# Two transformer blocks on one core: seven levels of a gated linear attention placed in pairs among the banks of the projections

## The reference

```python
b = jnp.cumsum(gi.astype(jnp.float32), axis=2)
diff = b[:, :, :, None, :] - b[:, :, None, :, :]
decay = jnp.exp(jnp.where(causal[None, None, :, :, None], diff, -jnp.inf))
A = jnp.einsum('bhid,bhjd,bhijd->bhij', qf, kf, decay)
o_intra = jnp.einsum('bhij,bhje->bhie', A, vf)
...
o_g = rms_norm(o_g, g_norm[l]).reshape(B, T, G_WIDTH) * jax.nn.silu(rg)
```

## Time and profile before

| what | value |
|---|---|
| median of three runs | 1561.66 us (1561.66 to 1562.43) |
| the profiled execution | 1561.91 us |
| its span, first to last instruction | 1560.1 us |
| PE busy | 1544.7 us |
| DVE busy | 991.2 us |
| ACT busy | 667.5 us |
| POOL busy | 504.8 us |
| granted clock of TensorE | 0.999 |

### The profile page before, as it was taken

The page is one execution under the profiler, slowest core; times in us unless marked ns, Lnnn a source line. Parts: engine busy times, 40 slices in busy tenths (PEclk is TensorE's granted clock), DMA queues, the critical chain, the costliest instruction groups (busy, mean ns, idle before and its releaser), DMA issues.

```text
span 1560.1 us, 20969 instructions
## 1 busy us (share of the span) xinstructions
PE 1544.7 (99%) x7728; PEld 1298.3 (83%) x7728; DVE 991.2 (64%) x1192; ACT 667.5 (43%) x1096; POOL 504.8 (32%) x285
## 2 busy tenths in 40 slices
PE   8999999999999999999999999999999999999998
PEld 6888888888788888888888898988888988888886
DVE  5464875435477777876664747357356677777776
ACT  5352565244444443443533334543334454434442
POOL 2451000000037776765410000020013037777761
PEclk9999999999999999999999999999999999999999
DMA  6422135221312223222332232343334222213232
GB/s 246 151 71 80 41 109 186 85 82 54 135 54 108 108 108 108 108 108 69 128 101 85 59 95 68 95 149 112 108 115 156 93 103 81 94 61 119 83 110 79
DMA packets 44709, 160.16 MB, mean 103 GB/s; under 512 B 5552, under 2 KB 5752, under 8 KB 44240
## 3 DMA queue, kind: packets, MB, share of 16 engines
q1 hardware_dynamic: 40608, 144.82, 28.3%
q0 software_dynamic: 4016, 14.18, 2.6%
HBM read 156.80 MB, written 3.76 MB: 103 GB/s over the span
## 4 chain that ended last, share of the span: by engine, by line
PE 93%; DVE 3%; ACT 2%; DMA 1%; issue 1%; POOL 0%; DVEq 0%; ACTq 0%; SPq 0%; POOLq 0%
PE banks L1237 29%; PE banks L1239 29%; PE banks L1238 29%; PE banks L1532 1%; PE banks L1411 1%; DVE nmax L2210 1%; DVE w_lo L1941 1%; DMA w_raw<-in_weights 1%; PE banks L1349 0%; PE banks L1594 0%; DVE banks L2209 0%; PE banks L1570 0%; PE banks L1562 0%; PE banks L1521 0%; ACT w_hi L1630 0%
## 5 line engine op out<-in xcount | busy, mean ns | idle before, releaser
L1237 PE MATMUL banks<-act_hi,w_hi 128*128 128x512 f32 (+1 forms) x1088 | 413.4, 380 | 3.1 <-DVE act_lo L2092 3.1
L1239 PE MATMUL banks<-act_hi,w_lo 128*128 128x512 f32 (+1 forms) x1088 | 410.0, 377 | 0.0
L1238 PE MATMUL banks<-act_lo,w_hi 128*128 128x512 f32 (+1 forms) x1088 | 409.9, 377 | 0.0
L1941 DVE TENSOR_TENSOR w_lo<-w_raw,w_hi 128x1024 fp32r<-128x1024 f32 x208 | 271.2, 1310 | 187.4 <-ACT w_hi L1630 186.4
L1630 ACT ACTIVATE w_hi<-w_raw 128x1024 fp32r<-128x1024 f32 x208 | 218.5, 1059 | 241.8 <-DMA w_raw<-in_weights 189.3
L1237 PEld LDWEIGHTS banks<-act_hi,w_hi 128*128 128x128 f32 x1088 | 204.8, 188 | 41.2 <-DVE w_lo L1941 1.6
L1239 PEld LDWEIGHTS banks<-act_hi,w_lo 128*128 128x128 f32 x1088 | 204.7, 188 | 37.7
L1238 PEld LDWEIGHTS banks<-act_lo,w_hi 128*128 128x128 f32 x1088 | 204.8, 188 | 36.5
L1237 PE MATMUL banks<-w_hi,a_hi 128*128 128x512 f32 x392 | 152.7, 390 | 0.0
L1238 PE MATMUL banks<-w_lo,a_hi 128*128 128x512 f32 x392 | 152.6, 389 | 0.0
L1239 PE MATMUL banks<-w_hi,a_lo 128*128 128x512 f32 x392 | 152.5, 389 | 0.0
(11 more groups left out here) (345 smaller groups left out, 2410.2 us busy)
## 6 DMA issues: line engine op xcount, KB each, us to landing
w_raw<-in_weights SPq DMA_DIRECT2D x208, 512.0 KB, 3.6
w_down<-in_weights SPq DMA_DIRECT2D x56, 512.0 KB, 6.4
wide<-share_dram POOLq DMA_DIRECT2D x3, 1024.0 KB, 10.7
x_tok<-in_x SPq DMA_DIRECT2D x4, 512.0 KB, 5.1
w_first<-in_weights SPq DMA_DIRECT2D x4, 512.0 KB, 8.2
x_tok<-in_x POOLq DMA_DIRECT2D x4, 512.0 KB, 5.4
out<-x_tok SPq DMA_DIRECT2D x8, 256.0 KB, 2.0
skew_dram<-bias_dram POOLq DMA_DIRECT2D x1, 1536.0 KB, 12.1
```

The costliest lines, as they stand in the source:

```text
L1237: pe.matmul(out_ap, lhs[0], rhs[0], start=start, stop=False, skip_group_check=goes_on)
L1238: pe.matmul(out_ap, lhs[0], rhs[1], start=False, stop=False, skip_group_check=goes_on)
L1239: return pe.matmul(out_ap, lhs[1], rhs[0], start=False, stop=stop, skip_group_check=goes_on)
L1941: dve.tensor_tensor(w_lo[:, slot, :], landed(kind, raw), w_hi[:, slot, :], ALU.subtract).then_inc(lo_w, 1)
```

## The change

The loop over the seven levels hands out the same ten banks in another rhythm, as (banks ahead of level 0, 1, ... 6): before 0, 1, 2, 2, 2, 2, 1; after 1, 0, 4, 0, 4, 0, 1.

```diff
@@ -598,7 +598,7 @@
                   s.bank_steps("va", "tok", "act", banks_at=(0, 1, 2, 0)))
     go(steps, 2)
     for n in range(last):
-        go(steps, 0 if n == 0 else 1 if n in (1, last - 1) else 2)
+        go(steps, 0 if n % 2 else 1 if n in (0, last - 1) else 4)
         s.levels[n] = s.add("level", SIDE[n % 2 * 2:n % 2 * 2 + 2], n=n, ready=all_out())
         if n == 0:
             s.add("farprep")
```

## The result

The changed kernel takes 1564.63 us (median of 22 runs, 1562.82 to 1565.47), beside 1561.84 us for the kernel before on the same chips (22 runs, 1561.35 to 1563.25). The ratio is 1.0015, with a 95% interval of 1.0009 to 1.0021: slower by 1.4 to 3.3 us by that interval, and by 2.8 us by the medians. That is little, and at the edge of what such a measurement can tell from no change. The forecast was 1563.5, in a range of 1561.0 to 1565.0.

The account below looks back on a forecast made before the run. PE, busy for 99% of the span, was taken as the bound. Three pairs' gaps, -0.6 us, plus a new 2.5 us stall gave +1.9 us, so a median of 1563.5 us, range 1561.0 to 1565.0.

Parts of the forecast that it names:

- The removed gaps: On PE, pairing levels drops one exit and one entry gap, 0.2 us per pair; three pairs give -0.6 us.
- The moved work: Levels 0 to 6 regrouped: each engine's work moves along; level 0 one bank later on PE, by 5.44 us.
- the need at 96.09: On PE, qa0's 19th matmul needs the last weight unit, unit 3, at 96.09 us.
- DVE's rigid shift: In the first pair, farprep's products move 5.44 us later: k_far's from 87.07 to 92.51, q_far's from 88.21 to 93.65.
- ACT's 92.4 and POOL's 93.6: Level 3's exponential follows k_far's on ACT at 92.4 us; POOL's first multiplication of level 3 starts at 93.6.
- The turns: DVE and POOL alternate at SBUF: q_far's multiplication ends 1.2 us late, unit 3's w_lo is ready at 98.4.
- The wait: PE stalls in qa0 for unit 3's w_lo; the loss is 2.5 us, paid in full, once.
- The small stall: Rival: DVE's two multiplications precede POOL's turn, w_lo ready at 97.2; net +0.7 us, 1562.4; chance 0.21.
- The large stall: Rival: unit 3's w_lo loses one more turn to POOL; net +2.9 us, 1564.6; chance 0.13.
- The second stall at ka0: Rival: the chain from level 2 to unit 3's split exceeds 11.4 us; measurably slower from 12.6 us; chance 0.09.
- no stall at all: Rival: level 1's copies and unit 3's split come over 1.2 us earlier; only gaps go, 1561.1; chance 0.1.
- a wait past 120 us: Sign that the prediction is wrong: PE's waits after the change include one past 120 us.

Follow-up runs that it names:

- the two kernels that keep all pairs and have no wait: Changed kernel with farprep moved behind rg3: 1560.76 us, ratio 0.9993; changed kernel with only qa's unit 3 split moved ahead of level 0: 1560.59 us, ratio 0.9993.
- the first profile: The profiled execution of the changed kernel itself, nothing else altered: 1564.91 us, span 1563.1.
- the eleven later runs: The changed kernel measured once more, unaltered, on the chip of the other experiments: 1564.21 us, ratio 1.0015 to the kernel before.
- the two kernels concerned: The changed kernel, profiled at 1564.91 and 1563.36 us, and the kernel before with only levels 0 and 1 paired, profiled at 1564.13, 1565.78 and 1568.82 us.

## Why the prediction was right, and where its sum was off

**The removed gaps: right in kind, too small.** I put the three pairs at -0.6 us. They give 1.1, by the start of level 6 in the two kernels that keep all pairs and have no wait, and 0.75 for two pairs. A level takes 1.93 us up to the next kind of matmul, but 32 matmuls of it inside a pair take less: two levels take 3.71 and not 3.86. The two rows show that the 1.93 up to the next kind holds some 0.15 us that are not spent between two levels; I had taken them for part of the level, from a row in which the next group was of transposes. So a pair gives 0.35 and not 0.2.

**The moved work: right to 0.1 us.** PE's order, the need at 96.09 (the due time was 95.96), DVE's rigid shift (k_far's product at 92.51, q_far's at 93.65, measured 92.51 and 93.66), ACT's 92.4 and POOL's 93.6 all came as worked out. That level 1's operands are no limit held, and no later unit was late: neither ka0 nor va0 has an entry among the waits.

**The turns: right.** One turn was lost at q_far's product (2.29 us), none at w_lo, and the low part was ready at 98.30 for a forecast of 98.4. Both were close: POOL's product began at 93.60 and q_far's at 93.66, w_lo at 97.09 and POOL's subtraction at 97.15, so that by the same turns 0.06 us the other way would have given the small or the large stall; no run shows these two orders by themselves. The kernel in which POOL comes later shows the price by itself: with its 1.22 us for the product the wait is 0.9 shorter. The Trainium skill (SBUF — State Buffer, Who interferes with whom) states that a VectorE instruction with two SBUF inputs contends with a GpSimd instruction that reads SBUF, and that one with at most one SBUF input, outside the 2-port modes, does not. The traces agree with both: the products of q_far and of level 3 take 2.29 and 2.25 us beside each other, for 1.22 and 1.27 alone, and the masked copies, whose data come from PSUM, take 1.32 to 1.36 us beside POOL.

**The wait: right, and its price incomplete.** The loss of 2.5 us by the wait and its long first step was measured as 2.4 + 0.1. That it is paid in full holds as well, and that it is paid only once up to the 0.2 us at kx named below. The term that was missing is what the clock does in and behind the wait. My sum counted a late PE as late, but running at full speed from there on. In the first profile 1.5 us more were lost at 0.50 of the clock; in the profile of the same kernel at 1563.36 us none. The sum of the measured terms is -1.1 + 2.5 = +1.4 without and +2.9 with it. The runs lie in two such groups, 9 of 22 up to 1563.62 and 13 from 1564.17, whose medians (1563.31 and 1564.91) are 1.5 and 3.1 us over before, and the median of all falls into the upper one. The mean clock of each run goes with it: 0.999 or 1.000 in all nine and 0.998 in all 13, where some 3 us at the lower level are 0.001 of the span. In the eleven later runs one of the upper group, 1565.07, shows 1.000 all the same. My 1563.5 owes its closeness to two errors of opposite sign: 0.5 too little gain for the pairs, and 1.5 too little loss for the clock in the runs where it falls.

**The rivals.** The small stall (DVE ahead of POOL) did not come by itself, but was made, and gave +0.4 us by the medians and +0.5 by level 6, for the +0.7 worked out. The large stall's time, 1564.6, is the one measured, by another mechanism than the one named. The second stall at ka0 did not come. Its unit 3 was ready at 123.02 for a matmul at 125.73, 2.7 us in time where 1.2 to 1.9 were worked out:

```profile
121.30 1.72 DVE L1941 TENSOR_TENSOR w_lo<-w_raw,w_hi 128x1024 fp32r<-128x1024 f32 x1 [3.71 <-ACT w_hi L1630]
125.73 0.39 PE L1237 MATMUL banks<-act_hi,w_hi 128*128 128x512 f32 x1
```

That there is no stall at all was made in two ways, and gives 1560.6 to 1560.8. One sign of being wrong came in name only: a wait past 120 us, the 0.2 us for a copy of kx past 200 us. PE's weight load waits for that copy in every kernel, 0.2 us before and 0.3 to 0.6 where there is a wait at unit 3; what links the two was not followed up.

**What stays open.** Why the same wait of 2.2 us is followed by a half clock in one execution and not in the next is not settled, nor why it ends after 3 us in one and after 10 in another. Nor is it the change alone that brings a low clock: two of the 22 runs of the kernel before beside the later ones, 1563.21 and 1565.64, have a mean clock of 0.998 and 0.997. In the five profiles of the two kernels concerned the wait itself is 2.23 or 2.24 us, so the length of the wait does not tell them apart; what does was not found. In the three with a low stretch the clock fell some 0.15 us ahead of the late matmul twice, and 0.6 us behind it once.

## What to carry to other kernels

When steps are regrouped, look for the instruction whose place in a side engine's list moves behind a block of work, and set its end against the bank that needs it: here one split was 2.4 us late, while all the grouping was worth 1.1. The repair that keeps the gain is to move that one instruction ahead. Where PE is the bound, a new wait of two microseconds can cost more than its length, since the clock may halve inside or behind it; a sum for such a change should carry that term as a case of its own.

## What the runs showed of the hardware that was not expected

A wait of PE of 1.3 us (1.5 against the due time) was followed by full clock in its profile, and its 11 runs lie within 1.5 us, all with a mean clock of 0.999 or more. A wait of 2.2 was followed by full clock in two profiles and by the lower level in three, lasting some 3 us in two of them and 10 us in one. In those of 3.65 and 4.43 the clock fell to the lower level before PE was back, at 99.8 and 99.0 for matmuls at 100.06 and 100.84, and all six runs of each lie above 1565.8, with a mean clock of 0.997 or 0.998. In the two longer low stretches the clock came back only at 105.8 (with the wait of 4.43) and 109.4, while PE was working without a gap; and in the one that ended at 109.4 it had fallen at 99.2, when PE had been at work again since 98.64.
